# Sixteen experts of 128 rows each become experts of 96 rows, computed in two column halves and four column quarters of the matmul array

## The reference, cut to what matters

```python
scores = jax.nn.sigmoid(h @ w_router)                       # 576 tokens x 16 experts
biased = scores + router_bias
grp_top = lax.top_k(biased.reshape(T, 4, 4), 2)[0]          # best 2 of each of 4 groups
group = jnp.argmax(grp_top.sum(-1), axis=-1)                # best group
masked = jnp.where(expert_group == group, biased, -inf)
_, idx = lax.top_k(masked, 2)                               # top 2 inside it
...
for e in range(16):
    he = jax.nn.silu(h @ w_gate[e]) * (h @ w_up[e])         # 1024 -> 256
    y = y + gates[:, e:e + 1] * (he @ w_down[e])            # 256 -> 1024
```

## Time and profile before

| | |
|---|---|
| median of 3 runs (range) | 1231.68 us (1231.42 to 1232.84) |
| profiled execution, first to last instruction | 1232.1 us |
| TensorE busy | 1110.6 us (90%) |
| VectorE, ScalarE, GpSimd busy | 507.9, 281.4, 93.6 us |
| mean granted TensorE clock | 0.951 |
| expert stages (first row transpose to last store) | 226.7 to 413 us, 1004.6 to 1191 us |

### The profile page before, as it was taken

One profiled execution on the slowest core, in us unless ns is written; L12 is line 12 of the kernel. 1 busy time (PEld: TensorE's weight loads), 2 busy tenths in 40 slices (PEclk: granted clock), 3 DMA queues, 4 the chain that ended last, 5 costly groups with the idle time before them and its releaser, 6 DMA issues.

```text
span 1232.1 us, 19092 instructions
## 1 busy us (share of the span) xinstructions
PE 1110.6 (90%) x7210; PEld 674.8 (55%) x7210; DVE 507.9 (41%) x1320; ACT 281.4 (23%) x681; POOL 93.6 (8%) x115
## 2 busy tenths in 40 slices
PE   7999995699999489999899998999999849999985
PEld 3586453344444246677788876555555424444432
DVE  1570336011111383479635554665523611111118
ACT  0102013111111121423244332354411321111110
POOL 0010002000000300000121111210000110000011
PEclk9999997799999789999999998999999869999997
DMA  9469008999994544122322242745510599999535
GB/s 350 205 231 195 1 1 318 359 339 361 381 368 159 202 128 148 35 88 78 89 76 75 71 135 75 288 160 217 218 69 1 218 349 358 362 369 379 234 115 192
DMA packets 85378, 246.26 MB, mean 200 GB/s; under 512 B 9488, under 2 KB 50496, under 8 KB 66720
## 3 DMA queue, kind: packets, MB, share of 16 engines
q1 hardware_dynamic: 64304, 153.15, 34.1%
q0 software_dynamic: 11760, 58.24, 13.2%
q10 hardware_dynamic: 9216, 33.56, 7.6%
HBM read 205.63 MB, written 58.16 MB: 214 GB/s over the span
## 4 chain that ended last, share of the span: by engine, by line
PE 86%; DVE 5%; DMA 4%; issue 3%; POOL 1%; ACT 1%; POOLq 0%; DVEq 0%; SPq 0%; ACTq 0%
PE bank L1213 18%; PE bank L1149 11%; PE bank L1233 9%; PE bank L1383 9%; PE bank L1301 5%; PE bank L1480 4%; PE bank L1319 3%; PE bank L1355 3%; PE bank L1203 2%; DMA ring<-in_stream_dram 1%; PE bank L1733 1%; PE bank L1758 1%; PE bank L1163 1%; DMA xrows<-x,rowi 1%; PE bank L1460 1%
## 5 line engine op out<-in xcount | busy, mean ns | idle before, releaser
L1149 PE MATMUL bank<-ring,cat 128*128 128x512 f32 (+1 forms) x320 | 140.5, 594 | 1.4 <-ACT cat L1902 1.4
L1213 PE MATMUL bank<-ring,work 128*128 128x512 f32 x256 | 113.8, 596 | 0.0
L1383 PE MATMUL bank<-xT,ring 128*128 128x288 f32 x448 | 110.9, 407 | 0.0
L2324 DVE TENSOR_TENSOR work<-work,bank 128x256 f32<-128x256 f32 x32 | 13.5, 421 | 218.7 <-ACT work L1873 218.7
L1383 PEld LDWEIGHTS bank<-xT,ring 128*128 128x128 f32 x448 | 84.6, 190 | 24.1 <-issue 1.5
L1149 PEld LDWEIGHTS bank<-ring,cat 128*128 128x128 f32 (+1 forms) x320 | 56.1, 179 | 74.8 <-issue 74.8
L1213 PEld LDWEIGHTS bank<-ring,work 128*128 128x128 f32 x256 | 48.0, 193 | 54.1 <-issue 54.1
L1203 PE MATMUL bank<-const,work 128*128 128x128 f32 x256 | 36.4, 292 | 32.1 <-DMA work<-xrows 32.1
L1301 PE MATMUL bank<-xT,ring 128*128 128x288 f32 x256 | 63.1, 407 | 0.0
L1873 ACT ACTIVATE work<-bank 128x256 f32<-128x256 f32 x32 | 12.3, 385 | 207.5 <-PE bank L1213 207.5
L1203 PEld LDWEIGHTS bank<-const,work 128*128 128x128 f32 x256 | 32.8, 152 | 47.2 <-DMA work<-xrows 32.4
(11 more groups left out here) (432 smaller groups left out, 1803.7 us busy)
## 6 DMA issues: line engine op xcount, KB each, us to landing
ring<-in_stream_dram SPq DMA_DIRECT2D x71, 1024.0 KB, 7.3
cat<-in_stream_dram SPq DMA_DIRECT2D x16, 1024.0 KB, 8.9
work<-xrows ACTq DMA_DIRECT2D x32, 512.0 KB, 5.6
xT<-in_stream_dram SPq DMA_DIRECT2D x16, 1024.0 KB, 8.7
work<-in_stream_dram SPq DMA_DIRECT2D x16, 1024.0 KB, 9.8
yrows<-work ACTq DMA_DIRECT2D x32, 512.0 KB, 6.0
by_batch<-in_pages_dram SPq DMA_DIRECT2D x128, 128.0 KB, 2.4
xrows<-work POOLq DMA_DIRECT2D x1, 8192.0 KB, 27.4
```

What stands on the lines that cost most here:

```text
L1149: i = pe.matmul(bank(n)[0:ROWS[tile], :], cat[:, k, tok(tile)], slot(w[k // 4], 4, 512)[:, k % 4, :], start=(k == 0), stop=(k == KC - 1))
L1213: i = pe.matmul(bank(n), xgT[:, e % 2, k, :], sparse_slot(layer, 3 * e + k // 4, 4, 512)[:, k % 4, :], start=(k == 0), stop=(k == KC - 1))
L1383: i = pe.matmul(bank(n + s)[:, 0:nn], slot(w, KC, 256)[:, k, P * (m % 2):P * (m % 2) + P], xT[:, k, a:a + nn], start=(k == 0), stop=(k == ...
```

## The change

The row tables give an expert 96 rows (CAP) in place of 128, and the flag goes to the general path above 96. Transposes and row loads handle 96 rows. The first 64 rows (WIDE) of an expert and the last 32 (THIN) are then computed apart. For the wide rows, a matmul has 64 stationary columns; it is issued twice, once for each half of the array's columns, and each half gets its own half of the weight columns. For the thin rows it has 32 stationary columns and is issued four times, for four quarters of the array and of the weight columns. So GU's outputs take 384 columns of the bank: 2 x 128 for wide, 2 x 64 for thin. HT becomes a transpose of 128 columns and one of 64, and its copy on ACT three copies that put the pieces in their places. D0 is now the thin rows' down projection (256 bank columns) and D1 the wide rows' (512). A result store becomes two DMAs, with rows cut into 2 KB (wide) and 1 KB (thin) pieces, and each wait on the stores counts 32 where it counted 16.

```diff
+WIDE, THIN = 64, 32
+CAP = WIDE + THIN
+PART = D_EXP // 2 + D_EXP // 4
...
-            pool.dma_start(xrows[0:N_EXP * P].rearrange("(e p) d -> p e d", p=P), zero.unsqueeze(1).broadcast_to([P, N_EXP, D_MODEL]))\
+            pool.dma_start(xrows[0:N_EXP * CAP].rearrange("(e p) d -> p e d", p=CAP),
+                           zero[0:CAP].unsqueeze(1).broadcast_to([CAP, N_EXP, D_MODEL]))\
...
-                            i = pe.transpose(bank(n, 4, P)[:, k, :], xg[:, e % NXG, P * (4 * g + k):P * (4 * g + k + 1)], ident)
+                            i = pe.transpose(bank(n, 4, CAP)[:, k, :],
+                                             xg[0:CAP, e % NXG, P * (4 * g + k):P * (4 * g + k + 1)], ident[0:CAP, 0:CAP])
...
-                    for k in range(KC):
-                        i = pe.matmul(bank(n), xgT[:, e % 2, k, :],
-                                      sparse_slot(layer, 3 * e + k // 4, 4, 512)[:, k % 4, :],
-                                      start=(k == 0), stop=(k == KC - 1))
+                    by_half = bank(n, 2, PART)
+                    for rows, at in ((WIDE, 0), (THIN, WIDE)):
+                        parts = P // rows
+                        width = D_EXP // parts
+                        to = 0 if rows == WIDE else D_EXP // 2
+                        for k in range(KC):
+                            w = sparse_slot(layer, 3 * e + k // 4, 4, 2, D_EXP)[:, k % 4]
+                            for q in range(parts):
+                                i = pe.matmul(by_half[rows * q:rows * q + rows, :, to:to + width],
+                                              xgT[:, e % 2, k, at:at + rows], w[:, :, width * q:width * q + width],
+                                              start=(k == 0), stop=(k == KC - 1))
...
-                    for k in range(2):
-                        i = pe.transpose(bank(n, 4, P)[:, k, :], hS[:, e % 2, P * k:P * k + P], ident)
+                    pe.transpose(bank(n)[:, 0:P], hS[:, e % 2, 0:D_EXP // 2], ident)
+                    i = pe.transpose(bank(n)[0:D_EXP // 4, P:2 * P], hS[:, e % 2, D_EXP // 2:PART], ident)
...
-                    for half in range(2):
-                        n = ejob(layer, e, f"D{half}")
+                    for kind, rows, at in (("D0", THIN, WIDE), ("D1", WIDE, 0)):
+                        parts = P // rows
+                        width = D_MODEL // parts
+                        n = ejob(layer, e, kind)
                         claim(pe, n)
                         for k in range(2):
-                            i = pe.matmul(bank(n), hTS[:, e % 2, k, :],
-                                          sparse_slot(layer, 3 * e + 2, 2, D_MODEL)[:, k, 512 * half:512 * half + 512],
-                                          start=(k == 0), stop=(k == 1))
+                            w = sparse_slot(layer, 3 * e + 2, 2, D_MODEL)[:, k]
+                            for q in range(parts):
+                                i = pe.matmul(bank(n)[rows * q:rows * q + rows, 0:width], hTS[:, e % 2, k, at:at + rows],
+                                              w[:, width * q:width * q + width], start=(k == 0), stop=(k == 1))
...
-                        act.dma_start(xg[:, e % NXG, :], xrows[P * e:P * e + P, :]).then_inc(xg_loaded[layer][e % NXG], 16)
+                        act.dma_start(xg[0:CAP, e % NXG, :], xrows[CAP * e:CAP * e + CAP, :]).then_inc(xg_loaded[layer][e % NXG], 16)
...
-                        act.dma_start(yrows[P * e:P * e + P, :], yS[:, e % NYS, :]).then_inc(y_stored[layer][e % NYS], 16)
+                        wide = yrows[CAP * e:CAP * e + WIDE].rearrange("r (q f) -> q r f", q=P // WIDE)
+                        thin = yrows[CAP * e + WIDE:CAP * e + CAP].rearrange("r (q f) -> q r f", q=P // THIN)
+                        act.dma_start(wide, yS[:, e % NYS, 0:512]).then_inc(y_stored[layer][e % NYS], 16)
+                        act.dma_start(thin, yS[:, e % NYS, 512:768]).then_inc(y_stored[layer][e % NYS], 16)
...
-                            give(act.copy(xgT[:, (e + 1) % 2, 0:4, :], bank(n, 4, P)), n)
+                            give(act.copy(xgT[:, (e + 1) % 2, 0:4, 0:CAP], bank(n, 4, CAP)), n)
...
-                            give(act.copy(hTS[:, (e - 1) % 2, :, :], bank(n, 2, P)), n)
+                            to = hTS[:, (e - 1) % 2]
+                            act.copy(to[:, :, 0:WIDE], bank(n)[:, 0:P].rearrange("p (k r) -> p k r", k=2))
+                            thin = bank(n)[0:D_EXP // 4, P:2 * P].rearrange("p (k s r) -> p k s r", k=2, s=2)
+                            for s in range(2):
+                                i = act.copy(to[HD * s:HD * s + HD, :, WIDE:CAP], thin[:, :, s])
+                            give(i, n)
...
-                            act.activation(hgS, bank(n)[:, 0:D_EXP], ACT.Silu).then_inc(silu_done[layer], 1)
+                            act.activation(hgS, bank(n)[:, 0:PART], ACT.Silu).then_inc(silu_done[layer], 1)
...
-                            give(act.copy(yS[:, (e - 1) % NYS, 0:512], bank(n)), n)
+                            give(act.copy(yS[:, (e - 1) % NYS, 512:768], bank(n)[:, 0:256]), n)
...
-                    step(dve.tensor_scalar(s1[:, 0:1], s1[:, 0:1], float(P), None, ALU.is_gt))
+                    step(dve.tensor_scalar(s1[:, 0:1], s1[:, 0:1], float(CAP), None, ALU.is_gt))
...
-                            give(dve.tensor_copy(yS[:, (e - 1) % NYS, 512:], bank(n)), n)
+                            give(dve.tensor_copy(yS[:, (e - 1) % NYS, 0:512], bank(n)), n)
```

More of the change, by code:

```diff
@@ L79, in constant_table @@
     put("ones", np.ones((P, P)))
-    put("rowbase", np.tile(P * np.arange(N_EXP) * 1.0, (P, 1)))
+    put("rowbase", np.tile(CAP * np.arange(N_EXP) * 1.0, (P, 1)))
     i = np.arange(P)[:, None] % CH
@@ L740, in program @@
         o += NYS * D_MODEL
-        hgS = view(work, o, D_EXP)
+        hgS = view(work, o, PART)
         hS = view(work, o + D_EXP, 2, D_EXP)
@@ L750, in program @@
         crowded = ctx.enter_context(nc.sbuf_tensor("crowded", [1, 1], mybir.dt.int32))
-        xrows = nc.dram_tensor("xrows", [(N_EXP - 1) * P + P * NT, D_MODEL], F32).ap()
-        yrows = nc.dram_tensor("yrows", [N_EXP * P, D_MODEL], F32).ap()
+        xrows = nc.dram_tensor("xrows", [(N_EXP - 1) * CAP + P * NT, D_MODEL], F32).ap()
+        yrows = nc.dram_tensor("yrows", [N_EXP * CAP, D_MODEL], F32).ap()
         o = 0
@@ L997, in pool_mixture @@
                     for i in range(NYS):
-                        pool.wait_ge(y_stored[layer][i], 16 * ((N_EXP - 1 - i) // NYS + 1))
+                        pool.wait_ge(y_stored[layer][i], 32 * ((N_EXP - 1 - i) // NYS + 1))
                     for tile in range(NT):
@@ L1883, in mixture @@
                             if e - 1 >= NYS:
-                                act.wait_ge(y_stored[layer][(e - 1) % NYS], 16 * ((e - 1) // NYS))
+                                act.wait_ge(y_stored[layer][(e - 1) % NYS], 32 * ((e - 1) // NYS))
                             take(act, n)
-                            give(act.copy(yS[:, (e - 1) % NYS, 0:512], bank(n)), n)
+                            give(act.copy(yS[:, (e - 1) % NYS, 512:768], bank(n)[:, 0:256]), n)
                     store_rows(N_EXP - 1)
@@ L2319, in mixture @@
                             take(dve, n)
-                            give(dve.tensor_copy(xgT[:, (e + 1) % 2, 4:8, :], bank(n, 4, P)), n)
+                            give(dve.tensor_copy(xgT[:, (e + 1) % 2, 4:8, 0:CAP], bank(n, 4, CAP)), n)
                         if 0 <= e < N_EXP:
@@ L2323, in mixture @@
                             dve.wait_ge(silu_done[layer], e + 1)
-                            give(dve.tensor_tensor(hS[:, e % 2, :], hgS, bank(n)[:, D_EXP:], ALU.mult), n)
+                            give(dve.tensor_tensor(hS[:, e % 2, 0:PART], hgS, bank(n)[:, PART:2 * PART], ALU.mult), n)
                         if e > 0:
@@ L2327, in mixture @@
                             if e - 1 >= NYS:
-                                dve.wait_ge(y_stored[layer][(e - 1) % NYS], 16 * ((e - 1) // NYS))
+                                dve.wait_ge(y_stored[layer][(e - 1) % NYS], 32 * ((e - 1) // NYS))
                             take(dve, n)
-                            give(dve.tensor_copy(yS[:, (e - 1) % NYS, 512:], bank(n)), n)
+                            give(dve.tensor_copy(yS[:, (e - 1) % NYS, 0:512], bank(n)), n)
                     landed(dve, ejob(layer, N_EXP - 1, "D1") - NBANK + 1, NBANK)
```

## The result

The kernel after takes 1307.95 us (median of 4 runs, 1305.72 to 1313.15) against 1232.12 for the one before: a ratio of 1.062 [1.060, 1.064]. The forecast was 1164, 68 us less. It is 76 us slower instead.

What follows compares the result with a forecast made beforehand. PE was taken to set the pace. Steps of 9.20 against 11.39 us save 35.05 per stage; with stage-end, store, front and weight terms 33.8, two stages 67.6: 1231.7 - 67.6 = 1164 us, range 1146 to 1184.

Steps and rivals of the forecast that it cites:

- Rival (b): Thin rounds on PE: quarters with different moving weights run two at a time, step 11.81, total 1248 us; chance 0.05.
- (c): Expert matmuls on PE: columns don't pair at all for these operands, step 22.2, total 1578 us; chance 0.02.
- (d): An expert has more than 96 rows, so the general path runs: 48 us per expert, +586; chance 0.02.
- the clock (e): PE in the expert stages: the clock falls with tiles of a part of the array; no chance of its own.
- The second store issue (0.33) lies beside it as well: ACT inside a step: the added store issue takes 0.33 us and is free beside GU.
- An expert now moves 3.15 + 0.39 + 0.39 = 3.93 MB: DMA traffic per expert step: 3.93 MB in 9.20 us, which would be 427 GB/s.
- 1 us per stage for weights: Late in each expert stage: PE's wait for weight loads, taken as 1 us at a rate near 385 GB/s.
- The store waits now count two DMAs, issued two steps (18 us) earlier: Waits on result stores inside the expert stages: listed among the ACT and DVE work, with no time added.
- rival (a): Late in each expert stage: DMA becomes the bound, 8 us in place of 1, total 1178 us; chance 0.21.
- slow end: Loads needed before GU(15): at 368 GB/s 53.3 MB take 145 us, so PE waits about 5 us, perhaps 8.
- the last store: End of each expert stage: second DMA issued 0.33 later but smaller, put at +0.15 us (bounds -0.3 and +0.5).
- SP's waits for PE: Sign expected in the trace after: SP's waits for PE shrink from 119 us to some tens.

Runs made afterwards that it cites:

- 1: The kernel after, with each result store as six DMAs, one per column part (two of 64 pieces, four of 32), in place of two: 1187.68 us, 0.963 of before.
- 2 to 4: The kernel before, with layer 1's store cut to outermost dimension 2, 4 or 8 in place of 128: 1332.07, 1260.36 and 1235.22 us.
- 6: Kernel 1, but layer 1's weight blocks from the sixth on load only their first half: 1178.80 us, 0.956 of before.
- 7: Kernel 1, but layer 1 stores an expert in one flat DMA of 128 x 3 KB: 1178.74 us, 0.956 of before.
- 8: Kernel 1, but the four thin pieces are issued once D0 has landed, ahead of the wait for D1: 1182.98 us, 0.961 of before.

## Why the prediction was wrong

**PE: right.** A step of 9.25 against 9.20 (9.24 in the later kernels), with the terms where they were put, but for T (0.71, not 0.66): 32 thin matmuls from 249.19 to the next group at 250.09 are 0.028 each, so rounds of four at 0.11, though all four quarters stream different weights. Rival (b) falls. The limit of about 62 ns per MATMUL that the Trainium skill ("TensorE: Matmul & The Clock Gate", section "Wait — 56ns, not 53.3ns?") states for a PE whose hardware decoding is off would, by the estimate in the prediction, have given a step of 11.56; at 0.028 us per matmul it did not act here. Rivals (c) and (d) fall too: (c) needs 22.2 us of work in every step, and more than half take 9.2 to 9.8; (d) needs some 48 us. Inside the stages the clock (e) fell only behind holes that ACT had made.

**The step that failed** is the one on ACT and the stores: "The second store issue (0.33) lies beside it as well". The duration was that of an issue with 128 rows outermost, carried over to patterns with 2 and 4 outermost, which no row showed. A figure carried over like that needs bounds, and this one had none: it was priced as one more of the same instruction. It lasts up to 11.8 us, behind it on ACT stand the D0, T and HT copies, and PE has to wait in every second step. The same omission is in the DMA part. "An expert now moves 3.15 + 0.39 + 0.39 = 3.93 MB" spreads the 0.39 over sixteen engines; the wide rows' two thirds of it went over two of them. Shown by 1 (same bytes, -120 us) and by 2 to 4 (the shape alone, +99, +27, +2). None of the rivals held this cause; slower in any way had a chance of 0.09.

**Two more terms were mis-sized,** to be read in kernel 1, where the failed step is taken out and which still stands 24 us above the forecast. The first is the late stall. The sum has 1 us per stage for weights; beyond 9.2 the last three steps are 6.2 and 8.8, so 13 us more in all. What PE waits for is not the weights but the result stores: "The store waits now count two DMAs, issued two steps (18 us) earlier" was given no price, and late in the stage the stores land after 21 to 23 us. Behind it stands the capacity that rival (a) argued from: the "slow end" of 368 GB/s, discounted as a rate that PE's gating had set, is about what this mix gets when the DMAs are full (366 to 374 GB/s at a share of 1.02). (a) had the capacity right and the wait wrong. That its 1178 is also where 6 and 7 lie says nothing for it: they are other kernels. The second term is the last store. It was put at +0.15 per stage and costs +1.7 with six issues (4.57 from issue to gather, before 2.88), +0.25 with the order of 8. Together these are 16 of the 21 us by which the profiled execution of kernel 1, 1184.95, exceeds the forecast. Of the other 5, 0.7 is the copies of the last HT (PE idles 1.24 and 1.23, where 0.51 + 0.4 was put), and 1.2 the second step of the first stage (8.8, in the second stage 7.6); the rest is not assigned: its own runs spread over 4.4.

**A sign was badly chosen.** SP's waits for PE were to shrink "from 119 us to some tens", with the DMAs near full. They are 96.2 in kernel 1, whose DMAs are full, and 151.9 in the kernel after. SP waits whenever the ring's eleven slots are taken, and a slot whose load is still under way is taken too; so its waits are no measure of spare capacity, and in the earlier trace rows they were read as if they did.

**What remains open.** Why ACT's issue blocks just there (how many packets an engine's queue takes) was not measured. Whether more result buffers would take the late stalls away was not tried. A single store with rows outermost would need a source that steps partitions in an inner dimension, and was not tried. Best of the kernels that compute the whole is 8, at 0.961 of before: the change is worth its 4% once its stores are cut along the rows.

## What to carry to other kernels

Read the outermost dimension of both patterns of a DMA before pricing it: with 2, 4 and 8 it was the number of DMA engines here, and the cost is about the load of the busiest one, compared with the time that the compute engine needs. A DMA issue is only as cheap as its queue is short, so ask what stands behind it on the engine that issues it. A store must have landed before its buffer is needed again, so hold the measured time to landing against that distance. When compute gets faster, take the measured GB/s of the same mix of piece sizes as capacity, not that of pure loads, and load ahead no more than leaves the first rows a free path.

## What the runs showed of the hardware

- A store of 128 x 4 KB pieces costs 0.33 to 0.98 us of the issuing engine with 128 outermost, up to 1.3 with 8, 7.4 with 4 and 17.7 with 2, beside a full weight stream. A row load issued on the same queue waits too: its issue took at most 0.45 us before, 13.8 in the kernel after and 20.1 with 2, and its median time to landing rose from 5.6 us to 37 with 2 (1040 to 1120 us).
- When the DMA engines were full (share 1.02), six small stores per expert took 21 to 23 us to land, where they took 3 to 5 with half of the weights (share 0.83).
- In the kernel after, steps alternated between 9.2 and 20 us; the stage (227.8 us) met the estimated load of the busiest engine (226).
- Four column quarters with four different moving operands run side by side in float32 at 0.028 us per matmul, and four changes of the tile shape cost the 0.56 us per step put down for them. The Trainium skill ("TensorEngine Tiling (Array Packing)", section "Key Properties") says that a change of mode drains the engine, without a price; 0.14 us each fits the 9.25.
- The 24 matmuls behind a hole of 8.34 us on PE ran at a granted clock of 0.62 and took 4.47 us, not 2.91:

```profile
309.10:313.40 4.30, 4.30 (x24) 1.29 (x24) 0.35 (x1) 0.23 (x1) 0.00 (x0) 0.62 0.44 146
250.90:253.80 2.90, 2.90 (x36) 0.94 (x24) 0.35 (x1) 0.33 (x1) 0.00 (x0) 1.00 1.03 427
```
